# Mean and variance of each retention head summed by TensorE instead of GpSimd

## The reference

```python
def rms_norm(x, g):
    xf = x.astype(jnp.float32)
    y = xf * lax.rsqrt(jnp.mean(xf * xf, axis=-1, keepdims=True) + EPS)
    return (y * g.astype(jnp.float32)).astype(x.dtype)
...
def trunk_layer(x, r0, c0, pos, ...):
    h = rms_norm(x, g_mix_pre)
    proj = h @ w_in
    q, k, v, g_ret, ca, cb, ga, gb = jnp.split(proj, offs, axis=-1)
    q = rope(q.reshape(B, T, N_RET_HEADS, RET_DK), pos)
    k = rope(k.reshape(B, T, N_RET_HEADS, RET_DK), pos) * (RET_DK ** -0.5)
    o, r_new = retention_chunkwise(q, k, v, r0)
    o = layer_norm(o, ret_gn_gain.reshape(N_RET_HEADS, RET_DV))
    y_ret = (jax.nn.silu(g_ret) * o) @ w_ret_out
    u = ca * jax.nn.sigmoid(cb)
    z = lax.conv_general_dilated(padded, conv_w[:, None, :], ..., feature_group_count=D_CONV) + conv_b
    z = jax.nn.silu(layer_norm(z, conv_ln_g, conv_ln_b))
    y_conv = z @ w_conv_out
    merged = jax.nn.sigmoid(ga + b_ga) * y_ret + jax.nn.sigmoid(gb + b_gb) * y_conv
    x = x + rms_norm(merged @ w_o, g_mix_post)
    h2 = rms_norm(x, g_ffn_pre)
    f = (jax.nn.silu(h2 @ w_ffn_gate) * (h2 @ w_ffn_up)) @ w_ffn_down
    x = x + rms_norm(f, g_ffn_post)
```

## Time and profile before

| what | value |
|---|---|
| median of 3 runs | 1720.37 us (1720.36 to 1720.39) |
| the profiled execution | 1719.3 us |
| its span | 1717.5 us |
| TensorE's mean granted clock | 0.978 of 2.4 GHz |
| busy: TensorE, VectorE, ScalarE, GpSimd | 1638.5, 1187.7, 678.6, 347.0 us |

### The profile page before, as it was taken

One profiled execution on the slowest core, in us unless ns is written; L12 is line 12 of the kernel. 1 busy time (PEld: TensorE's weight loads), 2 busy tenths in 40 slices (PEclk: granted clock), 3 DMA queues, 4 the chain that ended last, 5 costly groups with the idle time before them and its releaser, 6 DMA issues.

```text
span 1717.5 us, 29871 instructions
## 1 busy us (share of the span) xinstructions
PE 1638.5 (95%) x10808; PEld 1573.4 (92%) x10808; DVE 1187.7 (69%) x1666; ACT 678.6 (40%) x966; POOL 347.0 (20%) x354
## 2 busy tenths in 40 slices
PE   6899999999799979999989999999997999999997
PEld 5898999999799959999979999999997998999997
DVE  6998778796947587554446978786877675555544
ACT  4323324151535434334343324151533554533433
POOL 6961202122210594000000402112130100000000
PEclk8999999999999989999999999999998999999999
DMA  6354746655344405444434556657463443344443
GB/s 246 112 191 142 259 160 214 211 182 197 124 132 138 170 11 164 153 148 156 152 116 161 187 175 208 212 181 233 148 209 100 136 158 111 113 151 153 147 160 109
DMA packets 73833, 275.94 MB, mean 161 GB/s; under 512 B 8272, under 2 KB 8272, under 8 KB 72688
## 3 DMA queue, kind: packets, MB, share of 16 engines
q1 hardware_dynamic: 52560, 192.17, 34.2%
q0 software_dynamic: 21152, 82.18, 13.4%
HBM read 230.43 MB, written 43.89 MB: 160 GB/s over the span
## 4 chain that ended last, share of the span: by engine, by line
PE 81%; DVE 10%; issue 6%; ACT 1%; POOL 0%; DMA 0%; DVEq 0%; ACTq 0%
PE bank L402 22%; PE bank L403 21%; PE bank L404 21%; PE bank L542 5%; PE bank L550 2%; DVE acc L1028 2%; DVE wlo L993 2%; PE bank L551 2%; PE bank L559 1%; DVE acc L1011 1%; PE bank L436 1%; DVE x L1287 1%; DVE tmp L1285 1%; PE bank L516 1%; PE bank L490 1%
## 5 line engine op out<-in xcount | busy, mean ns | idle before, releaser
L402 PE MATMUL bank<-hhi,whi 128*128 128x320 f32 x2016 | 657.8, 326 | 14.7 <-DVE wlo L993 13.5
L404 PE MATMUL bank<-hhi,wlo 128*128 128x320 f32 x2016 | 626.0, 311 | 0.0
L403 PE MATMUL bank<-hlo,whi 128*128 128x320 f32 x2016 | 625.6, 310 | 0.0
L993 DVE TENSOR_TENSOR wlo<-wring,whi 128x1024 fp32r<-128x1024 f32 x363 | 469.3, 1296 | 213.9 <-ACT whi L736 186.9
L402 PEld LDWEIGHTS bank<-hhi,whi 128*128 128x128 f32 x2016 | 381.8, 189 | 30.9 <-DVE wlo L993 15.8
L403 PEld LDWEIGHTS bank<-hlo,whi 128*128 128x128 f32 x2016 | 381.7, 189 | 12.3 <-issue 4.2
L404 PEld LDWEIGHTS bank<-hhi,wlo 128*128 128x128 f32 x2016 | 380.9, 189 | 0.0
L736 ACT ACTIVATE whi<-wring 128x1024 fp32r<-128x1024 f32 x264 | 277.5, 1055 | 243.8 <-PE bank L404 243.7
L1028 DVE SCALAR_TENSOR_TENSOR acc<-up,par,acc 128x256 f32<-128x256 f32 x480 | 260.8, 607 | 0.0
L1059 DVE SCALAR_TENSOR_TENSOR state<-state,con,bank 128x512 f32<-128x512 f32 x128 | 93.9, 747 | 109.9 <-PE bank L551 109.9
L766 ACT ACTIVATE whi<-wring 128x1024 fp32r<-128x1024 f32 x96 | 101.2, 1054 | 172.4 <-PE bank L404 164.2
(11 more groups left out here) (156 smaller groups left out, 2229.4 us busy)
## 6 DMA issues: line engine op xcount, KB each, us to landing
wring<-w SPq DMA_DIRECT2D x364, 512.0 KB, 3.3
state<-r_in POOLq DMA_DIRECT2D x64, 512.0 KB, 5.4
rs_out<-state POOLq DMA_DIRECT2D x64, 512.0 KB, 4.0
rp_out<-pst POOLq DMA_DIRECT2D x8, 512.0 KB, 6.4
us<-c_in POOLq DMA_DIRECT2D x2, 1216.0 KB, 5.7
cs_out<-us POOLq DMA_DIRECT2D x2, 1216.0 KB, 9.8
cp_out<-up POOLq DMA_DIRECT2D x2, 1144.0 KB, 5.9
con<-consts POOLq DMA_DIRECT2D x1, 1420.0 KB, 9.1
```

The source lines that it names most:

```text
L402: pe.matmul(bank[g][:, 0:T], whi[j][:, k, :], hi, start=start and k == 0, stop=False)
L403: pe.matmul(bank[g][:, 0:T], whi[j][:, k, :], lo, start=False, stop=False)
L404: mm = pe.matmul(bank[g][:, 0:T], wlo[j][:, k, :], hi, start=False, stop=stop and k == n - 1)
L993: return dve.tensor_tensor(dst, value, hi.bitcast(F32), ALU.subtract)
```

## The change

GpSimd's four adds for each head go, and the semaphore `head_sum` with them. TensorE multiplies each of the four feature tiles by `ones_v` and accumulates them in one bank, for the mean directly from `oT` and for the variance from the four tiles of squares in `sqo`. The variance's matmuls wait for ScalarE's squares (`sq_done`). Nothing else differs. Behind the edits on GpSimd the line numbers are smaller by 12, behind `late_var` by 9.

```diff
--- before.py
+++ after.py
@@ -188,7 +188,7 @@
         h_value, h_hi, h_ready = sem("h_value"), sem("h_hi"), sem("h_ready")
         dup_ready, kd_ready, khl_step, ks_ready = sem("dup_ready"), sem("kd_ready"), sem("khl_step"), sem("ks_ready")
         vs_hi = sem("vs_hi")
-        head_sum, conv_sum = sem("head_sum"), sem("conv_sum")
+        conv_sum = sem("conv_sum")
         g_hi, g_ready = sem("g_hi"), sem("g_ready")
         z_hi, z_ready = sem("z_hi"), sem("z_ready")
         m_hi, m_ready = sem("m_hi"), sem("m_ready")
@@ -287,13 +287,6 @@
                     pool.wait_ge(dve_aux, (l * HEADS + hd) * AUX_DVE + (3 + 2 * b + 2))
                     s = b % RING
                     pool.dma_start(rs_out[(l * HEADS + hd) * DB + b], state[s][:, :, :]).then_inc(r_stored[s], 16)
-                    if b == DB - 1:
-
-                        pool.wait_ge(act_aux, (l * HEADS + hd) * AUX_ACT + 5)
-                        pool.wait_ge(stat_read, l * STATS + (hd + (ST_X + 1)))
-                        pool.tensor_tensor(sqo[:, 0:2, :], oT[:, 0:2, :], oT[:, 2:4, :], ALU.add).then_inc(head_sum, 1)
-                        pool.wait_ge(head_sum, (l * HEADS + hd) * 4 + 1)
-                        pool.tensor_tensor(sqo[:, 0, :], sqo[:, 0, :], sqo[:, 1, :], ALU.add).then_inc(head_sum, 1)
                     if b and not (last and b > RING):
 
                         pool.wait_ge(r_stored[(b - 1) % RING], (l * HEADS + hd) * 32 + 16 * ((b - 1) // RING + 1))
@@ -304,11 +297,6 @@
 
                 pool.wait_ge(act_aux, (l * HEADS + hd) * AUX_ACT + 7)
                 pool.dma_start(rp_out[l * HEADS + hd], pst[:, :, :]).then_inc(pst_stored, 16)
-
-                pool.wait_ge(sq_done, l * SQS + (hd + (SQ_RET + 1)))
-                pool.tensor_tensor(sqo[:, 0:2, :], sqo[:, 0:2, :], sqo[:, 2:4, :], ALU.add).then_inc(head_sum, 1)
-                pool.wait_ge(head_sum, (l * HEADS + hd) * 4 + 3)
-                pool.tensor_tensor(sqo[:, 0, :], sqo[:, 0, :], sqo[:, 1, :], ALU.add).then_inc(head_sum, 1)
             def sum_of_squares(l):
 
                 pool.tensor_tensor(sqz[:, 0:4, :], sqz[:, 0:4, :], sqz[:, 4:8, :], ALU.add).then_inc(conv_sum, 1)
@@ -567,15 +555,18 @@
                 pe.wait_ge(act_aux, H * AUX_ACT + 5)
                 pe.wait_ge(stat_read, l * STATS + (hd + (ST_X + 1)))
 
-                pe.wait_ge(head_sum, H * 4 + 2)
-                pe.matmul(aux[A_MEAN % 3][:, 0:T], ones_v[:, :], sqo[:, 0, :], start=True, stop=True).then_inc(aux_done, 1)
+                for e in range(4):
+                    mm = pe.matmul(aux[A_MEAN % 3][:, 0:T], ones_v[:, :], oT[:, e, :], start=(e == 0), stop=(e == 3))
+                mm.then_inc(aux_done, 1)
 
             def late_var(l, hd):
                 H = l * HEADS + hd
                 aux_free(H, A_VAR)
 
-                pe.wait_ge(head_sum, H * 4 + 4)
-                pe.matmul(aux[A_VAR % 3][:, 0:T], ones_v[:, :], sqo[:, 0, :], start=True, stop=True).then_inc(aux_done, 1)
+                pe.wait_ge(sq_done, l * SQS + (hd + (SQ_RET + 1)))
+                for e in range(4):
+                    mm = pe.matmul(aux[A_VAR % 3][:, 0:T], ones_v[:, :], sqo[:, e, :], start=(e == 0), stop=(e == 3))
+                mm.then_inc(aux_done, 1)
 
             def late(l, hd, j, k):
```

## The result

The changed kernel takes **1732.45 us** in the median of 4 runs (1730.06 to 1735.0), against 1720.36 us before (4 runs, 1719.1 to 1720.39). The ratio is 1.0076, with a 95% interval of 1.0062 to 1.0089, so 13.1 us slower by the ratio and 12.1 by the medians. The forecast was 1734.0 in a range of 1729 to 1740. The profiled execution took 1732.24 us over a span of 1730.5 us, 13.0 us more than the span before. Lines behind the edits have new numbers: L402 is now L390, L571 is L559, L578 is L568, L668 is L659, L1028 is L1019, L331 is L319.

A forecast was written before the change was run, and what follows sets the result against it. TensorE was taken to bound heads 1 to 3, VectorE the last head's gb stage. +19.4 us of matmuls less 2 x 2.9 us gives +13.6 us; on the 1720.37 us median the forecast is 1734.0 us, range 1729 to 1740.

The forecast's parts named there:

- What bounds it: TensorE never waits in heads 1 to 3; beside the last head's gb units VectorE is the clock and TensorE has slack.
- The price, 0.54 us: Each of 48 added TensorE matmuls costs 0.54 us; 36 are paid, +19.4 us, and 12 in the last heads are covered.
- The rival of 0.15 us: Further matmuls onto the same bank cost one pass, 0.15 us each, so the kernel is not slower: 1717.6 us; chance 0.04.
- tipping point: Price of an added matmul at which the change would cause no loss, put near 0.25 us each.
- The relief, 5.5 us per layer: Without GpSimd's adds, VectorE's taps in gb units 4 and 6 speed up by 2.24 + 3.25 = 5.5 us per layer.
- the net 2.9 us: After the wait on the mean, everything up to the pair sum and its TensorE matmul comes 2.9 us sooner per layer.
- The wait on the mean: In the last head VectorE idles 2.5 us for four mean matmuls and starts the centring 0.3 us later than before.
- The margins: Reciprocal root and stored prompt state each arrive 0.9 us before VectorE needs them; TensorE has at least 0.3 us left.
- The total: +19.4 us paid on TensorE less 2.9 us gained in each of two layers: +13.6 us.
- By the page: By the skill's rule on VectorE and GpSimd excluding each other, removed adds return 5.0 us, not 5.5; sum 1.0 us higher.

The follow-up runs named there:

- e2: Against the kernel before, TensorE sums mean and variance of heads 0 to 2 only, the last head keeps GpSimd's adds: 1739.91 us, ratio 1.0111.
- e3: Kernel before with all GpSimd adds kept, the one matmul at each of the 16 places issued four times: 1740.7 us, ratio 1.0115.
- e1: Against the kernel before, TensorE sums mean and variance of each layer's last head only: 1714.18 us, ratio 0.9962.
- e4: As e1, with convolution taps moved so VectorE has work while waiting for the mean: 1709.29 us, ratio 0.994 to the kernel before.
- e5: Against the kernel before, TensorE sums only the mean of each layer's last head, GpSimd keeps the adds of squares: 1720.68 us, ratio 1.0.
- e6: Against the kernel before, TensorE sums only the squares of each layer's last head, GpSimd keeps the mean's adds: 1716.98 us, ratio 0.9982.
- e7: As e4, with TensorE's matmul for the convolution's mean one round later: 1696.17 us, ratio 0.986 to the kernel before.

## Why the prediction was right

- **What bounds it.** TensorE as the clock in heads 1 to 3: shown by e2 (36 more matmuls cost 19.1 us) and e3 (48 cost 19.8, so the 12 in the last head next to nothing). VectorE as the clock in the gb stage: shown by e1, where TensorE gets more to do and the kernel is faster. The prediction let VectorE work "without a pause" up to 467.6 us; it has one, of 0.24 us at 453.38, which changes no term.
- **The price, 0.54 us.** The group of four measures 2.15 us, 0.54 a piece, and each head 3.21 us against the 3.24 of the sum. The rival of 0.15 us fell. Its tipping point was mis-summed: with three more matmuls in each of two waits it is 13.6 / 42 = 0.32 us below 0.54, near 0.22 us and not 0.25.
- **The relief, 5.5 us per layer.** The taps came back to 2.46 and 3.25 us against 2.45 and 3.27. That it exists is shown by e3 beside the full change. That more than the net 2.9 us can be used is shown by e4: 2.4 us more per layer, so 5.3 of the 5.5; its whole gain, 10.3 us in two layers, fits this, though it also holds the moved last tap and the slower pair sum, which cancel.
- **The wait on the mean.** 2.48 us against 2.5, and the net of -2.9 per layer is -2.93. e5 shows that it takes what the first two adds give.
- **The margins.** The root came 0.84 us ahead (0.9 predicted), and no wait for the stored prompt state appeared. The pair sum ran in the idle time, and ended 0.02 us before the centring.
- **The total.** Forecast +13.6, measured +13.1 by the ratio, 13.0 in the spans. The stage that pays and the stage that gains were each within 0.7 us (e2: 19.1 for 19.4; e1: 6.5 for 5.8).
- **By the page.** The prediction set 5.0 us by the rule of the Trainium skill (SBUF — State Buffer, "Who interferes with whom") against 5.5 us by the rows. That comparison was uneven, for the 5.5 contain the pair sum and the 5.0 do not. With it the three GpSimd instructions beside the taps of unit 6 last 4.27 us, where the taps lost 3.25; the first two last 2.50, where the taps lost 2.24. The wait on the mean takes what the first two give, so by the rule the sum would have been, as an estimate, 19.4 + 2 x (0.3 - 4.27) = +11.5 us and not +14.6. The interval (10.7 to 15.3) excludes neither. One meeting alone, in e6, cost more than the GpSimd instruction lasted, 1.78 us for 1.59, and the others less, so the duration is a fair price but not an exact one.

Less sharp was the term for the pair sum in e6: an overlap of 1.2 us was charged, while the meeting cost 1.78.

## What to carry to other kernels

Sums moved to the tensor engine are free only where it waits. Price the added matmuls from the distance of starts, and split the places by which engine is the clock in each: here the same edit cost 3.2 us in three heads and earned 2.9 in the fourth, and doing it in the fourth alone beats both kernels. Where an engine is freed, look at what it then waits for; filling that wait (e4) and then moving the wait that was left (e7) took the gain from 6.5 us (e1) to 10.3 and then 24, each against the kernel before of its group.

## What the runs showed of the hardware

Which of VectorE and GpSimd gives way when both work from SBUF is not fixed. In the gb stage of the kernel before and in e6 VectorE did: of the six tap instructions beside one meeting the longest lasted 2.10 us in the first and 2.27 us in the second, and the median 0.48 and 0.47. (In the first a second tap, beside the second add, lasted 1.08 us.)

```profile
424.25 2.10 DVE L1028 SCALAR_TENSOR_TENSOR acc<-up,par,acc 128x256 f32<-128x256 f32 x1
```

```profile
L1048 DVE SCALAR_TENSOR_TENSOR acc<-up,par,acc x6: 471/472/2265, 429.4 to 433.2; 128x256 f32<-128x256 f32 x6
```

In e4 GpSimd did. Its pair sum of 1.57 us in quiet took 2.92 us, and the twelve taps of that stretch, four of them beside it, took 0.48 us each, unslowed:

```profile
429.71 2.92 POOL L340 TENSOR_TENSOR pairs<-pairs,acc 128x640 f32<-128x640 f32 x1
```

```profile
L1048 DVE SCALAR_TENSOR_TENSOR acc<-up,par,acc x12: 476/477/479, 426.4 to 430.7; 128x256 f32<-128x256 f32 x12
```

Its 1.35 us of excess are about the time from its start at 429.71 to the end of the taps at 431.19: it was held over some three of them, although each tap is an instruction of its own. e7 repeats it, 2.92 us in both layers. GpSimd is also the one held at the end of the chain, beside VectorE's `wlo`: the last pair sum takes 2.45 us in the kernel before and 3.58 in e4 beside two of them, against 1.57 in quiet, while `wlo`, which had begun first (467.44 us in the kernel before), keeps its 1.2 us. This pair sum is on the path, so the meeting costs about 0.9 us per layer there. By the Trainium skill's page (SBUF — State Buffer, "SBUF: two separate sides") the one that starts first has the pair of ports for its whole instruction; that GpSimd waits through several of VectorE's instructions goes beyond it. Nor do the records of the stretched taps agree with it: the tap of 424.25 began before the add (424.50), that of 430.18 before the pair sum (430.56), and both were the ones that gave way. What decides which side wins was not settled. The moment within a tap does not sort the cases: VectorE gave way where GpSimd's instruction began 0.14 us (195.31 in the kernel before), 0.24 us and 0.38 us into a tap, and GpSimd where it began 0.18 us into one (e4). No run varied the moment at which the two meet alone.

Single runs of one kernel spread by up to 5 us: the full change took 1730.06 to 1735.0. Three of the first four runs of the kernel before lay within 0.03 us; its later ones took 1717.5 to 1722.9, and one of them 1730.8. No experiment was made on that.
